# Gated linear attention prepared inside the attention loop, one operation a head and step

## The reference

```
gq, gk, gv, gg, gaf, gab, cval, cgate, aq, ak, av = split(h @ w_in)
la = log_sigmoid(ga @ gla_a_w + gla_a_b) / 16              # forward and backward
o_gla = rms_norm(o_f + flip(o_b)) * silu(gg)               # gated linear attention
u = silu(group_layer_norm(dwconv(cval * sigmoid(cgate))))  # convolution
o_att = softmax attention over context and latent keys
x = x + gate1 * (concat([o_gla, u, o_att]) @ w_out)
x = x + gate2 * peer(rms_norm(x))                          # expert retrieval
```

```
q_dec = q * exp(bc);  k_dec = k * exp(-bc)
a = where(lower, q_dec @ k_dec.T, 0)
o = a @ v + q_dec @ state
state = state * exp(b_last) + (k * exp(b_last - bc)).T @ v
```

## Time and profile before

| | us |
|---|---|
| median of 3 runs (lowest, highest) | 4561.29 (4558.73, 4563.65) |
| the profiled execution, and its span in the trace | 4560.16, 4558.4 |
| TensorE, VectorE, GpSimd, ScalarE busy | 2964.4, 2789.8, 2699.0, 954.6 |
| mean granted TensorE clock (1 is 2.4 GHz, 0.5 is 1.2 GHz) | 0.817 |

### The profile page before, as it was taken

How to read it: one execution, slowest core, us unless ns; L and a number is a source line. 1 busy time by engine, 2 the same in 40 slices (tenths; PEclk the granted TensorE clock), 3 DMA queues, 4 the chain that set the end, 5 groups by cost and what they waited for, 6 DMA issues and landing times.

```text
span 4558.4 us, 50026 instructions
## 1 busy us (share of the span) xinstructions
PE 2964.4 (65%) x17354; PEld 1289.0 (28%) x17354; DVE 2789.8 (61%) x6337; ACT 954.6 (21%) x2379; POOL 2699.0 (59%) x2760
## 2 busy tenths in 40 slices
PE   6997855566655565666578968455556665555555
PEld 4565521122211221222134655111212122212111
DVE  3515457667676677667535363676667766766673
ACT  2134012212221222122121331122122212211221
POOL 3700027777777777777748000577777777777775
PEclk9998678777788877877789968788878778888878
DMA  6532239999999999999931102799999999999998
GB/s 217 182 113 94 84 141 409 409 409 407 404 408 404 405 406 406 406 405 403 403 128 35 38 3 83 298 409 408 409 404 403 406 402 409 402 408 406 405 405 349
DMA packets 471181, 1450.20 MB, mean 318 GB/s; under 512 B 54165, under 2 KB 131345, under 8 KB 470801
## 3 DMA queue, kind: packets, MB, share of 16 engines
q0 software_dynamic: 368640, 1342.34, 74.4%
q1 hardware_dynamic: 102290, 104.66, 7.1%
HBM read 1443.62 MB, written 3.21 MB: 317 GB/s over the span
## 4 chain that ended last, share of the span: by engine, by line
PE 26%; DMA 23%; DVE 22%; POOL 15%; issue 11%; DVEq 2%; ACT 1%; SPq 0%; ACTq 0%; POOLq 0%
PE ps L551 25%; DMA arena<-in_peer_u,expert_rows 13%; DVE arena L1454 9%; DMA arena<-in_peer_v,expert_rows 9%; POOL arena L526 7%; POOL arena L534 7%; PE ps L686 1%; DVE arena L1402 1%; DVE arena L1371 1%; DVE top_indices L1401 1%; DVE arena L1433 1%; DVE arena L1436 1%; DVE chosen_pair L1438 1%; DVE top_values L1404 1%; DVE best_positions L1401 1%
## 5 line engine op out<-in xcount | busy, mean ns | idle before, releaser
L551 PE MATMUL ps<-arena 64*64 64x512 f32 (+5 forms) x14768 | 2740.3, 679 | 1430.7 <-issue 1175.7
L1454 DVE CUSTOM_DVE_ANT_0 arena<-arena,ps 128x1024 f32<-128x1024 f32 x1280 | 1526.7, 1219 | 891.3 <-DMA arena<-in_peer_u,expert_rows 887.9
L551 PEld LDWEIGHTS ps<-arena 64*64 64x64 f32 (+2 forms) x14768 | 1136.7, 179 | 3018.4 <-issue 2904.8
L526 POOL DMA_INDIRECT arena<-in_peer_u,expert_rows x1280 | 1217.9, 952 | 686.0 <-issue 306.7
L534 POOL DMA_INDIRECT arena<-in_peer_v,expert_rows x1280 | 1211.0, 946 | 412.2 <-issue 358.2
L1184 ACT ACTIVATE arena<-constants,expert_weight 128x64 f32<-128x64 f32 x1280 | 380.3, 339 | 1402.5 <-PE ps L551 1378.5
L513 POOL MEMSET arena<- 128x5632 f32 x2 | 9.6, 4792 | 372.8 <-ACTq L257 372.8
L1299 DVE TENSOR_REDUCE score_max<-ps 128x1 f32<-128x640 f32 (+1 forms) x80 | 57.4, 718 | 246.8 <-PE ps L551 246.8
L506 POOL TENSOR_SCALAR arena<-arena,vec_columns 128x512 f32<-128x512 f32 x120 | 150.4, 1264 | 10.2 <-issue 10.2
L515 POOL MEMSET arena<- 128x2048 f32 x2 | 3.6, 1806 | 226.7 <-DVEq L257 226.7
L1111 ACT ACTIVATE arena<-ps 128x256 f32<-128x256 f32 x80 | 30.7, 384 | 457.8 <-PE ps L551 444.2
(11 more groups left out here) (162 smaller groups left out, 1819.2 us busy)
## 6 DMA issues: line engine op xcount, KB each, us to landing
arena<-in_ada_w SPq DMA_DIRECT2D x40, 1024.0 KB
arena<-in_peer_u,expert_rows POOLq DMA_INDIRECT x1280
arena<-in_peer_v,expert_rows POOLq DMA_INDIRECT x1280
arena<-in_w_in SPq DMA_DIRECT2D x32, 512.0 KB, 4.1
arena<-in_ada_w SPq DMA_DIRECT2D x4, 2048.0 KB, 18.7
arena<-in_w_out SPq DMA_DIRECT2D x4, 2048.0 KB, 7.6
arena<-in_peer_wq SPq DMA_DIRECT2D x2, 4096.0 KB, 18.7
peer_modulation<-modulation_rows SPq DMA_DIRECT2D x4, 1536.0 KB, 11.5
```

The costliest lines, as they stand in the source:

```text
L526: pool.indirect_dma_start(UR[:, k % RING, :], None, u_rows, bass.IndirectOffsetOnAxis(ap=rows[:, g % LIVE, k:k + 1], axis=0))\
L551: return pe.matmul(out, lhsT, rhs, start=start, stop=stop)
L1454: dve.tensor_tensor_reduce(out=UR[:, k % RING, :], in0=UR[:, k % RING, :], in1=pair(1), scale=1.0, scalar=0.0, op0=ALU.mult, op1=ALU.add, ...
```

## The change

The decays, exponentials and products of the four rows are cut into single operations, and each is put into a step of the attention loop. On VectorE row j's four decay parts start at the steps of `DECAY_AT` and its three products at those of `PRODUCT_AT`; on ScalarE its three exponentials start at those of `EXP_AT`. The absolute values, the first exponentials and the logarithm of the gates move to the loop's beginning (steps 2 to 10). The modulation products of layer 0 run in every third step instead of every fourth. The buffers get other places, so that they no longer lie on the attention's own.

In `gla` the transposes of the keys come first, half of them ahead of the convolution's means; the updates use four banks instead of eight; the convolution's reciprocals move between the masked products, behind the fourth and the eighth pair of masks; and the output's square root and reciprocal become a logarithm and an exponential on ScalarE.

```diff
         def in_attention(i):
-            n = IN_PROJECT + (i - 2) // 4
-            return n if i >= 2 and i % 4 == 2 and n < NC else None
+            n = IN_PROJECT + (i - 2) // 3
+            return n if i >= 2 and i % 3 == 2 and n < NC else None
+
+        DECAY_AT, EXP_AT, PRODUCT_AT = (12, 16, 23, 30), (16, 20, 27, 34), (20, 27, 34, 38)
+
+        def part_at(i, table, parts):
+            for j, first in enumerate(table):
+                if first <= i < first + parts:
+                    return j, i - first
+            return None
...
-                pool.memset(ST[:, :, :, :], 0.0).then_inc(S["st_zero"], 1)
+                pool.memset(at(16384, 3 * 1408), 0.0).then_inc(S["st_zero"], 1)
+                pool.memset(ST[3], 0.0).then_inc(S["st_zero"], 1)
...
             def gla(l):
-                for ct in range(2):
-                    wide(pair(ct), mean_mat, CX[:, ct, :]).then_inc(S["cx_mean"], 1)
-                for ct in range(2):
-                    pe.wait_ge(S["cx_sq"], 2 * l + ct + 1)
-                    wide(zp(ct), mean_mat, CSQ[:, ct, :]).then_inc(S["cx_var"], 1)
-                for i in range(4):
-                    if i < 2:
-                        pe.wait_ge(S["cx_sd"], 2 * l + i + 1)
-                    pe.wait_ge(S["qk_ready"], 4 * l + i + 1)
+                def kk_transposes(i):
                     for t in range(NT):
                         m = pe.transpose(zp(i)[:, P * t:P * t + P], KK[:, i, P * t:P * t + P], ident)
                     m.then_inc(S["kk_ps"], 1)
+                for i in range(2):
+                    kk_transposes(i)
+                for ct in range(2):
+                    wide(pair(ct), mean_mat, CX[:, ct, :]).then_inc(S["cx_mean"], 1)
+                for i in range(2, 4):
+                    pe.wait_ge(S["cx_cent"], 2 * l + i - 1)
+                    kk_transposes(i)
+                for ct in range(2):
+                    pe.wait_ge(S["cx_sq"], 2 * l + ct + 1)
+                    pe.wait_ge(S["kk_ready"], 4 * l + ct + 1)
+                    wide(zp(ct), mean_mat, CSQ[:, ct, :]).then_inc(S["cx_var"], 1)
                 pe.wait_ge(S["kk_ready"], 4 * l + 4)
                 for u, (i, ch, _n) in enumerate(UPD):
-                    if u >= 8:
-                        pe.wait_ge(S["st_ready"], NUPD * l + u - 7)
+                    if u >= 4:
+                        pe.wait_ge(S["st_ready"], NUPD * l + u - 3)
...
+                pe.wait_ge(S["cx_sd"], 2 * (l + 1))
                 pe.wait_ge(S["st_ready"], NUPD * (l + 1))
...
-                    if 8 <= i < 12:
+                    if 2 <= i < 6:
...
-                    if i == NS + 2:
+                    if i == 10:
                         act.activation(LZ[:, :, :], LZ[:, :, :], ACT.Ln, bias=1.0).then_inc(S["ln_done"], 1)
+                    if part_at(i, EXP_AT, 3):
+                        j, part = part_at(i, EXP_AT, 3)
+                        if part == 0:
+                            act.wait_ge(S["b_ready"], 4 * l + j + 1)
+                            act.activation(QD[:, j, :], LA[:, j, :], ACT.Exp, scale=1 / 16)
...
-                    act.activation(OSD[:, hp, :], pair(hp)[:, 0:NTOK], ACT.Sqrt, bias=eps_c[:, 0:1])\
-                        .then_inc(S["og_sd"], 1)
+                    st.link(act.activation(OSD[:, hp, :], pair(hp)[:, 0:NTOK], ACT.Ln, bias=eps_c[:, 0:1]))
+                    act.activation(OSD[:, hp, :], OSD[:, hp, :], ACT.Exp, scale=-0.5).then_inc(S["og_sd"], 1)
...
                     if 2 <= i < NS + 2 and i % 2:
                         evacuate(i - 2)
+                    if part_at(i, DECAY_AT, 4):
+                        decay(*part_at(i, DECAY_AT, 4))
+                    if part_at(i, PRODUCT_AT, 3):
+                        decayed(*part_at(i, PRODUCT_AT, 3))
...
                     ins.then_inc(S["atm_ready"], 1)
+                    if s in (3, 7):
+                        conv_scaled(s // 4)
                 for hp in range(2):
                     dve.wait_ge(S["og_sd"], 2 * l + hp + 1)
-                    st.link(dve.reciprocal(OSD[:, hp, :], OSD[:, hp, :]))
```

More of the change, by code:

```diff
@@ L157, in build @@
         LZ = at3(21504, 4, NTOK)
-        ST = A[:, 12544:18176].rearrange("p (i s e) -> p i s e", i=4, s=11)
+        ST = [A[:, i:i + 1408].rearrange("p (s e) -> p s e", s=11) for i in (16384, 17792, 19200, 27904)]
         LA = at3(0, 4, NTOK)
-        KK = at3(20736, 4, NTOK)
-        QD = at3(18176, 4, NTOK)
-        KD = at3(23296, 4, NTOK)
+        KK = LZ
+        QD = at3(12800, 4, NTOK)
+        KD = [at(i, NTOK) for i in (26624, 27264, 31744, 32384)]
         KKT = A[:, 35064:37624].rearrange("p (i t f) -> p i t f", i=4, t=NT)
[L165 to L169, removed]
+        ATM = A[:, 25472:26496].rearrange("p (r h d i) -> p r h d i", r=2, h=2, d=2)
+        OG = at3(21504, 2, NTOK)
+        OSQ = at3(22784, 2, NTOK)
+        OSD = at3(24064, 2, NTOK)
+        CSQ = at3(2560, 2, NTOK)
         WOUT = [at3(0, 4, D), at3(12288, 4, D)]
@@ L1068, in gla, with keys_out @@
             def gla(l):
+                def keys_out(i):
+                    act.wait_ge(S["kk_ps"], 4 * l + i + 1)
+                    act.activation(KKT[:, i, :, :], zp(i)[:, 0:NTOK].rearrange("p (t f) -> p t f", t=NT), ACT.Copy)\
+                        .then_inc(S["kk_ready"], 1)
+                act.wait_ge(S["mod_out"], 64 * stored(NC))
+                for i in range(2):
+                    keys_out(i)
                 for ct in range(2):
@@ L1316, in normalise, with decay, decayed @@
                        prec[:, :].unsqueeze(2).to_broadcast([P, 8, 64]), ALU.mult).then_inc(S["o_ready"], 1)
+                def decay(i, part):
+                    b = QD[:, i, :]
+                    bch = b.rearrange("p (c s) -> p c s", c=NCH)
+                    lch = LA[:, i, :].rearrange("p (c s) -> p c s", c=NCH)
+                    kch = KK[:, i, :].rearrange("p (c s) -> p c s", c=NCH)
+                    total = bch[:, :, CHUNK - 1:CHUNK].to_broadcast([P, NCH, CHUNK])
+                    if part == 0:
+                        dve.wait_ge(S["ln_done"], l + 1)
+                        st.do(stt(LA[:, i, :], LA[:, i, :], 0.0, LZ[:, i, :], ALU.min, ALU.subtract))
+                    elif part == 1:
+                        st.after(st.n)
+                        st.do(dve.tensor_tensor_scan(b, scan_keep, LA[:, i, :], 0.0, ALU.mult, ALU.add))
+                    elif part == 2:
+                        st.after(st.n)
+                        st.do(dve.tensor_copy(e_last[:, i, :].unsqueeze(2), bch[:, :, CHUNK - 1:CHUNK]))
+                        if i < 2:
+                            st.do(tt(kch, total, bch, ALU.subtract))
+                        else:
+                            st.do(tt(kch, bch, lch, ALU.subtract))
+                    else:
+                        st.after(st.n)
+                        if i < 2:
+                            dve.tensor_copy(LA[:, i, :], b).then_inc(S["b_ready"], 1)
+                        else:
+                            tt(lch, total, kch, ALU.subtract).then_inc(S["b_ready"], 1)
+                def decayed(i, part):
+                    hp = i % 2
+                    if part == 0:
+                        dve.wait_ge(S["ex_done"], 4 * l + i + 1)
+                        st.do(stt(QD[:, i, :], GQ[:, hp, :], 0.125, QD[:, i, :], ALU.mult, ALU.mult))
+                    elif part == 1:
+                        st.do(tt(KD[i], GK[:, hp, :], KD[i], ALU.mult))
+                    else:
+                        st.do(tt(KK[:, i, :], GK[:, hp, :], KK[:, i, :], ALU.mult))
                 for i in range(NS + 3):
@@ L1326, in gla @@
             def gla(l):
-                for i in range(4):
-                    dve.wait_ge(S["ln_done"], l + 1)
-                    st.do(stt(LA[:, i, :], LA[:, i, :], 0.0, LZ[:, i, :], ALU.min, ALU.subtract))
-                st.after(st.n)
                 for ct in range(2):
@@ L1334, in gla, with conv_scaled @@
                     tt(CX[:, ct, :], CX[:, ct, :], pair(ct)[:, 0:NTOK], ALU.subtract).then_inc(S["cx_cent"], 1)
[L1335 to L1352 removed]
+                def conv_scaled(ct):
                     dve.wait_ge(S["cx_sd"], 2 * l + ct + 1)
```

67 lines of the change are left out of this document (20 added, 47 removed).

## The result

The changed kernel takes 4571.83 us (median of 19 runs, 4561.26 to 4617.78), the kernel before 4559.91 in the same set (19 runs, 4554.54 to 4563.65): ratio 1.0041, 95% interval 1.0022 to 1.0060. It is slower by 0.41%, where 4506.7 had been forecast. Four of the 19 runs lie between 4603 and 4618; no run of before is above 4564.

The account below looks back on a forecast made before the run. TensorE was taken to bound the attention loop, VectorE's uncovered preparation the stage behind it. Gains of 25.7 us (layer 0) and 28.9 (layer 1), together 54.6, gave 4505.6 profiled, 4506.7 as a median; range 4490 to 4532.

Parts of the forecast that it names:

- The preparation leaves the stage: Linear-attention stage: first state update 11.6 us into it instead of 39.87, gain 28.3 us a layer (26 to 28.7).
- the end: End of the linear-attention stage: logarithm and exponential replace square root and reciprocal, gain 3.8 us a layer (3 to 4.5).
- The convolution's reciprocals: Masked products: reciprocals delay the next mask pair 1.7 us, covered by TensorE's slow 4.1 us step; costed at nothing.
- four banks: State updates with four banks instead of eight: taken as nothing; as a rival, waits give 4525 us, chance 0.04.
- The 45 operations in the loop: Attention loop: 32 VectorE and 13 small ScalarE operations cost nothing, hidden by TensorE's 3.03 us step, except in four places.
- term (d): Short steps of the prompt's tile at the loop's end: six added operations cost 0.8 us a layer (0 to 4.9).
- Term (a): Step 10 of the attention loop, both layers: logarithm and table loads delay softmax, stalling TensorE 2.4 us (0 to 4.9).
- Term (b): Step 20, layer 0 only: a modulation product waits for ScalarE's evacuation of bank 7, 2.5 us (0 to 3.2).
- Term (c): Layer 0's attention loop: the first modulation product waits for its slab's transfer, 0.7 us once (0 to 6 x 0.7).
- slower: Rival: all added operations lie on the path, 38.5 us a layer, plus 4.9 at step 10; 4583 us, chance 0.03.
- the clock stays up: Rival: masked products keep 2.4 GHz, 24.4 us instead of 41.1, reciprocals then stall; about 4478 us, chance 0.09.
- ScalarE pauses around each table load: Rival: 1.28 us pauses at the end's four loads and step 10's two, 7.7 us a layer; 4522 us, chance 0.02.

Follow-up runs that it names:

- e7: e6 with five unused 128x512 products put between the updates and the masked products in both layers; 4485.73 us, ratio 0.9843.
- e6: e2 with layer 0's modulation products at every fourth step again, so none falls on step 20; 4492.34 us, ratio 0.9857.
- e1: The kernel before, with only an unused logarithm of four rows added on ScalarE at step 10 of the attention loop; 4625.0 us, ratio 1.0149.
- e3: The changed kernel with three unused 128x512 products on TensorE at step 11 of layer 1's loop, ahead of the waiting transposes; 4539.54 us, ratio 0.9934.
- e5: The changed kernel with 64 unused products shaped like modulation products at step 11 of layer 1, behind the transposes that waited; 4519.17 us, ratio 0.9923.
- e4: The changed kernel with step 10's logarithm split into four rows, at steps 10, 14, 21 and 28 of the loop; 4532.71 us, ratio 0.9941.
- e2: The changed kernel with the gates' absolute value, exponential and logarithm moved ahead of the loop, into the values projection; 4502.3 us, ratio 0.9909.
- e9: The changed kernel with only layer 0's modulation products at every fourth step again, logarithm still at step 10; 4560.97 us, ratio 1.0002.

## Why the prediction was wrong

- *The preparation leaves the stage*, 28.3 a layer, and *the end*, 3.8: right. 118.38 - 86.33 = 32.05 and 118.05 - 85.99 = 32.06, with the first update at 11.59 (11.6) and 11.66 behind the last product (11.5). (The chain written out there ends at 535.5, not 535.6; nothing hangs on it.)
- *The convolution's reciprocals, four banks*: nothing, as costed. e7 shows the cover that the text named: at the upper clock the reciprocal stalls TensorE.
- *The 45 operations in the loop*: nothing, as costed; in e6's layer 1 every step of the first four tiles is as long as before's, to 0.01 us, and the 0.8 us by which that loop is longer all lie in the prompt's tile, as term (d), 0.8, had it.
- **Term (a), the stall at step 10: this step failed.** Its length was right (2.54 for 2.4), its price was not. It was costed as idle time alone, "between 0 and 4.9", although the text had both levels of the clock and the 41 us at 0.50 before it. What it cost was the clock of the 29 steps behind it: 65.9 us in layer 1 for 2.4 + 0.8 forecast. e1 makes the loss with the stall alone, e3 keeps the stall of ScalarE and takes TensorE's idleness away, e5 keeps both and repairs the clock behind them.
- **Term (b), step 20**, failed in the same way, in some runs only: 2.40 us of wait for 2.5 forecast, and 38 more where the clock went (e3 against the changed kernel). The profiled executions of e3, e4 and e5 lost it there, those of e2 and the changed kernel did not. Why 2.4 us cost the clock in one execution and not in the next stays open. The Trainium skill (the same Part 1) reports of the rise of the clock that it varies from run to run; no run here shows that, and here it is the fall that varies.
- *Term (c), the slabs*: near. The first product to wait for its slab does so for 0.55 us in the changed kernel, for 0.7 forecast, but for 1.05 to 1.30 in e2 to e5, which have the same steps. That is inside the bounds given.
- The rival *slower* had the right side and the wrong mechanism: it charged the operations and the 4.9 us of (a). The rival *the clock stays up* looked at the clock in the stage only, and only upwards. No case had it falling in the loop, so the chances left it out altogether.
- *ScalarE pauses around each table load*: no. The logarithm at 2543.52 starts 0.02 us after its load has ended, in the loop as in the earlier trace rows, so the drain that the Trainium skill states ("ScalarE: Activation LUTs", "What ACT_TABLE_LOAD costs") isn't seen here either.

With the two gaps out of the way (e6) the change is worth 66.8 us, where the sum without (a), (b) and (c) would be 62.6.

## What to carry to other kernels

A stall of TensorE has two prices, its own length and the clock of what follows: multiply the work up to the next dense stretch by the ratio of its two rates (here 5.72 to 3.03 us a step) before costing a gap of 2.5 us at 2.5 us. A long operation with table switches on ScalarE belongs where TensorE waits for nobody, here in the values projection; where it can't go there, unused products in the gap (e3) or a burst behind it (e5) save most of it: loops of 144.95 and 148.63 us instead of 206.16. If TensorE is busier than before with the same number of instructions, read the granted clock first.

## What was not expected of the hardware

The same products hold a grant of 1.00 for a whole loop once they have it (57.00 of 57 us in e5) and stay at 0.50 for 140 us when they have not. Five products of 128x512 in 6.6 us raised it ahead of the masked products, and 32-column products in 4.72 us in the loop. The length of a pause doesn't tell by itself whether the clock goes. Behind 1.95 (e7), 2.41 (e3, e4, e5), 2.54 (changed kernel, e5, e9) and 3.16 us (e1) it went, but also behind 1.30 (e4, layer 0) and behind 0.74 with 0.15 ahead of it (e4, layer 1). Behind 2.40 (changed kernel, e2), 1.05 to 1.14 (e2, e3, e5), 0.94 and 0.89 (e4) it stayed. In the prompt's tile, where e6's layer 1 waits three times for 0.44 to 0.48 us within 8 us, the grant is 0.99 from 2606 to 2614 and 0.50 behind that, and the linear-attention stage then starts at the lower level.
